# Hybrid decoder layer on one core: the first layer of the NSA compression with its tokens stationary and its weights moving

## The chip, the cores and the metric

The kernel runs on one core of one Trainium2 chip. The metric is device time in microseconds for one execution of the whole layer, from the first to the last instruction; lower is better.

## The reference, cut to what matters

One decoder layer for 512 tokens of width 1024: a joint input projection feeds multi-head latent attention (MLA) and native sparse attention (NSA: selected, sliding-window and compressed branches), an output projection and a squared-ReLU MLP follow. The change lies in the compressed branch, which turns windows of 32 tokens (stride 16, so 31 windows) of keys (kv = 0) and values (kv = 1) into one token each by a small two-layer network:

```python
def compress(t, pe, w1, w2):           # t: keys or values, 2 groups (G) x 64 (Dh)
    c = t.reshape(B, n_chunk, CMP_STRIDE, G, Dh)
    blocks = jnp.concatenate([c[:, :-1], c[:, 1:]], axis=2)
    blocks = blocks + pe[None, None, :, None, :]
    flat = blocks.transpose(0, 1, 3, 2, 4).reshape(B, n_cmp, G, CMP_BLOCK * Dh)
    return jax.nn.silu(flat @ w1) @ w2          # w1: 2048 x 128, w2: 128 x 64
k_cmp = rms_norm(compress(keys), k_gain[0]);  v_cmp = compress(values)
```

## The kernel before, in words

TensorE (PE) turns, multiplies and accumulates in PSUM; ScalarE (ACT) and VectorE (DVE) split float32 operands into a high and a low fp32r half, run the softmax and empty PSUM; GpSimd (POOL) does inverse roots, row scalings and the DMAs that add; SyncE (SP) loads weights. Each weight slice ("piece") of 128 x 1024 float32 goes through one of three slots of `raw` (RAW = 3) in the order of PIECES (L109), so that piece n may be loaded only when piece n - 3 is done with (`raw_free`, L592).

The attention is a list of units (UNITS, L156). Engines run the loop over units n in step with each other: at step n, PE computes the scores of unit n (`score_unit`, it waits for DVE's `lows` of unit n - 2), then whatever else is put at that step, then the products with the values of unit n - 4 (`mix_unit`, or `mix_pair` for four units together, L2342), then it turns the probabilities of unit n - 2 (`turn_unit`, by the helper `turn`, L2133, which waits for ACT's exponential). DVE at step n adds bias and finds the maximum (L1568) and copies turned probabilities (L1580); ACT runs the exponential of unit n - 1 (L1119). The first 32 units are MLA's; u = n - 32 counts NSA's. This order is written out by hand.

Compression is dealt out to the steps by `compress(u)` on each engine:
- u = 0, 2, 4, 6 on PE: the raw keys and values of 128 tokens are turned; ACT (`top_taps`, L1205) and DVE (`low_taps`, L1722) copy them at u = 1, 3, 5, 7 to `tap_planes`, where partitions 0 to 63 hold a token and 64 to 127 the next one. A row of position embeddings stands at either end.
- u = 10 to 17 on PE: `hidden(kv, quarter)` (L2378), the first layer. w1 is stationary (128 x 128), the 64 windows (2 groups x 32) move past it. Four matmuls a visit, keys at u = 10 to 13, values at u = 14 to 17. Each takes a half of w1: pieces w1 0 and 1 are the halves for keys, 2 and 3 for values. Piece 0 is free after the visit at u = 11 (`taps_used`), piece 1 after the visit at u = 13 (`turned`).
- u = 14 and 18 on DVE: the sums are put together (L1764 to L1771); u = 15 and 19 on ACT: the exponential (L1252); u = 16 and 20, 21 on DVE: 1 + e, its reciprocal and the product, `hid_k` and `hid_v` (L1776 to L1789).
- The second layer: keys on PE at u = KC_AT = 19 (L2261), DVE's `kc_ss` at u = 19 (L1733 to L1737), POOL's inverse root, PE again at KT_AT = 25; values at VC_AT = 27. The compressed keys are first used at u = 28.

Between these steps PE turns MLA's output rows (`turn_mix`, MIX_AT: u = 9, 15, 20, 23; made by POOL's `mix_row_of`), and from u = 21 on it runs parts of the output projection at most steps (L2113 to L2115).

A float32 matmul (not fp32r) shows in the trace as two LDWEIGHTS and two MATMUL records; a float32 transposition as one of each.

## Time and profile before

| | |
|---|---|
| Median of 3 runs | 641.41 us (640.96 to 641.7) |
| The profiled execution's own time | 640.96 us |
| Its span | 639.1 us |
| Granted TensorE clock, mean | 1.0 of full speed |
| PE busy | 626.0 us (98%) |
| DVE busy | 496.3 us (78%) |
| ACT busy | 400.0 us (63%) |
| POOL busy | 172.3 us (27%) |

The profiled execution is one of the three. Shares are of the span; busy times of one engine are the union of its instructions, and a "xN" is a count of records.

### The profile page before, as it was taken

What the parts mean: (1) busy time and instruction counts of PE and PEld (TensorE: products, weight loads), DVE (VectorE), ACT (ScalarE), POOL (GpSimd) and SP (SyncE); (2) the same over time, 40 slices, a digit from 0 to 9 for tenths busy, and PEclk for the clock granted to TensorE, in tenths of its full rate; (3) what the DMA queues carried; (4) which work ended last, traced back from release to release, by engine and by line L of the source; (5) the groups of instructions that cost most, each with busy time, mean ns of one, the idle gap of its engine ahead of it and who ended that gap; (6) DMA issues with size and microseconds to landing.
All of it is one profiled execution on the core that took longest, in us unless ns stands there. A gap on an engine that the chain in (4) does not pass through costs nothing.

```text
span 639.1 us, 11631 instructions
## 1 busy us (share of the span) xinstructions
PE 626.0 (98%) x4105; PEld 553.2 (87%) x4105; DVE 496.3 (78%) x913; ACT 400.0 (63%) x791; POOL 172.3 (27%) x236
## 2 busy tenths in 40 slices
PE   7999999999999999999999999999999999999998
PEld 5999788887689888888899999999998788888886
DVE  6665756578887888887896787777778999987666
ACT  5864675567897647566457676666747566644462
POOL 5656656434322201122110111111112121222200
PEclk9999999999999999999999999999999999999999
DMA  9881629997998964897365688787877899999975
GB/s 337 279 307 71 260 69 341 301 286 209 248 269 253 367 205 165 264 265 165 55 145 183 174 222 236 194 220 203 205 175 170 211 237 241 241 222 257 258 233 174
DMA packets 34506, 142.49 MB, mean 223 GB/s; under 512 B 5159, under 2 KB 5543, under 8 KB 33488
## 3 DMA queue, kind: packets, MB, share of 16 engines
q1 hardware_dynamic: 22688, 83.72, 37.8%
q0 software_dynamic: 10208, 34.88, 29.5%
q10 hardware_dynamic: 1552, 23.14, 9.5%
q8 instruction: 33, 0.54, 0.3%
q14 instruction: 25, 0.20, 0.1%
HBM read 139.57 MB, written 65.06 MB: 320 GB/s over the span
## 4 chain that ended last, share of the span: by engine, by line
PE 87%; DVE 5%; ACT 3%; DMA 3%; issue 2%; POOL 1%; SPq 0%; ACTq 0%; DVEq 0%; POOLq 0%
PE bank L2113 15%; PE bank L2115 15%; PE bank L2114 15%; PE bank L2503 7%; PE bank L2505 7%; PE bank L2504 7%; PE bank L2133 7%; PE bank L2342 3%; PE bank L2285 2%; PE bank L2324 2%; DVE w_lo L1396 1%; PE bank L2296 1%; PE bank L2297 1%; DMA raw<-weights 1%; PE bank L2378 1%
## 5 line engine op out<-in xcount | busy, mean ns | idle before, releaser
L868 POOL DMA_DIRECT2D down_sums<-w_down x64 | 49.8, 779 | 230.8 <-PE bank L2505 138.8
L1396 DVE TENSOR_TENSOR w_lo<-raw,w_hi 128x1024 fp32r<-128x1024 f32 (+3 forms) x70 | 81.1, 1171 | 22.9 <-ACT w_hi L965 22.5
L2113 PE MATMUL bank<-w_hi,act_hi 128*128 128x512 f32 (+3 forms) x224 | 89.6, 400 | 3.0 <-DVE w_lo L1396 2.6
L965 ACT ACTIVATE w_hi<-raw 128x1024 fp32r<-128x1024 f32 (+3 forms) x70 | 68.5, 993 | 30.4 <-DMA raw<-w_pairs 22.5
L2115 PE MATMUL bank<-w_hi,act_lo 128*128 128x512 f32 (+3 forms) x224 | 79.7, 356 | 0.0
L2114 PE MATMUL bank<-w_lo,act_hi 128*128 128x512 f32 (+3 forms) x224 | 79.7, 356 | 0.0
L1119 ACT ACTIVATE p_buf<-s_buf,stats 128x128 f32<-128x128 f32 (+3 forms) x96 | 53.8, 561 | 32.3 <-PE bank L2133 17.3
L1357 ACT ACTIVATE w_hi<-raw 128x1024 fp32r<-128x1024 f32 x31 | 32.8, 1059 | 35.5 <-DMA raw<-down_sums 20.7
L2113 PE MATMUL bank<-w_hi,s_all 128*128 128x512 f32 x140 | 54.7, 390 | 0.0
L2114 PE MATMUL bank<-w_lo,s_all 128*128 128x512 f32 x140 | 54.5, 389 | 0.0
L2115 PE MATMUL bank<-w_hi,s_all 128*128 128x512 f32 x140 | 54.5, 389 | 0.0
L2113 PEld LDWEIGHTS bank<-w_hi,act_hi 128*128 128x128 f32 x224 | 42.2, 188 | 13.0 <-issue 5.1
L2503 PE MATMUL bank<-act_hi,w_hi 128*128 128x256 f32 x168 | 47.6, 283 | 1.6 <-DVE a_all L1908 1.6
L2505 PE MATMUL bank<-act_hi,w_lo 128*128 128x256 f32 x168 | 47.6, 283 | 0.0
L2505 PE MATMUL bank<-g_all,w_lo 128*128 128x256 f32 x168 | 47.6, 283 | 0.0
L2503 PE MATMUL bank<-g_all,w_hi 128*128 128x256 f32 x168 | 47.6, 283 | 0.0
L2504 PE MATMUL bank<-act_lo,w_hi 128*128 128x256 f32 x168 | 47.6, 283 | 0.0
L2504 PE MATMUL bank<-g_all,w_hi 128*128 128x256 f32 x168 | 47.5, 283 | 0.0
L2114 PEld LDWEIGHTS bank<-w_lo,act_hi 128*128 128x128 f32 x224 | 42.3, 189 | 5.9 <-issue 1.2
L2115 PEld LDWEIGHTS bank<-w_hi,act_lo 128*128 128x128 f32 x224 | 42.1, 188 | 5.4
L1996 DVE TENSOR_TENSOR w_lo<-raw,w_hi 128x1024 fp32r<-128x1024 f32 x31 | 37.8, 1218 | 11.0 <-ACT w_hi L1357 11.0
L2133 PE MATMUL bank<-consts,p_buf 128*128 128x128 f32 x248 | 45.0, 279 | 1.0 <-ACT m_k L1068 0.3
(317 smaller groups left out, 1809.1 us busy)
## 6 DMA issues: line engine op xcount, KB each, us to landing
down_sums<-w_down ACTq DMA_DIRECT2D x32, 512.0 KB, 6.0
down_sums<-w_down POOLq DMA_DIRECT2D x64, 256.0 KB, 5.6
raw<-down_sums SPq DMA_DIRECT2D x32, 512.0 KB, 5.4
up_sums<-w_pairs POOLq DMA_DIRECT2D x28, 512.0 KB, 9.3
raw<-up_sums SPq DMA_DIRECT2D x28, 512.0 KB, 4.6
raw<-weights SPq DMA_DIRECT2D x26, 512.0 KB, 6.3
up_sums<-w_pairs SPq DMA_DIRECT2D x16, 512.0 KB, 6.4
raw<-w_down SPq DMA_DIRECT2D x16, 512.0 KB, 5.2
```

Of the source, the lines that this page charges most:

```text
L868: pool.dma_start(sums_dram[k, rows_], a["w_down"][SUMS[m][1], step, rows_], accum_op=ALU.add, max_dma_last_dim=4096).then_inc(*sum_added[k ...
L965: ins = act.activation(hi[:, 0:width], raw[:, n % RAW, 0:width], ACT.Copy)
L1119: act.activation(p_buf[:, n % 2, 0:nk], s_buf[:, n % 2, 0:nk], ACT.Exp, scale=-1.0, bias=neg_max[:, m:m + 1], accum_out=den[:, d:d + 1]).t ...
L1396: ins = dve.tensor_tensor(lo[:, 0:width], raw[:, n % RAW, 0:width], hi[:, 0:width].bitcast(F32), ALU.subtract)
L1996: dve.tensor_tensor(lo, src, hi.bitcast(F32), ALU.subtract).then_inc(*lo_done.mark(JOBS[d]))
L2113: pe.matmul(dst, a_h, w_h, start=start, stop=False, skip_group_check=onto)
L2114: pe.matmul(dst, a_h, w_l, start=False, stop=False, skip_group_check=onto)
L2115: return pe.matmul(dst, a_l, w_h, start=False, stop=stop, skip_group_check=onto)
L2133: ins = pe.transpose(bank[0:m, i * step:i * step + k], tile, ident[0:k, 0:k])
L2503: pe.matmul(dst, h[:, k * P:(k + 1) * P], g_h[:, k, :], start=start and k == 0, stop=False, skip_group_check=onto)
L2504: pe.matmul(dst, h[:, k * P:(k + 1) * P], g_l[:, k, :], start=False, stop=False, skip_group_check=onto)
L2505: ins = pe.matmul(dst, l[:, k * P:(k + 1) * P], g_h[:, k, :], start=False, stop=k == KD // 2 - 1, skip_group_check=onto)
```

## The change

Stationary and moving change places. A matmul now has 64 windows (for one kv) as its stationary operand, 128 x 64, read from `tap_planes` at every 8th element, and 128 columns of w1 move. Keys' sums go to partitions 0 to 63 of a PSUM bank, values' to 64 to 127, the two alternating as `mix_pair` does. The eight visits become four, at u = 10, 11, 13 and 14, of eight matmuls each (four for keys, four for values); the visits at 10 and 11 take both first halves of w1, those at 13 and 14 both second halves, and the pieces are ordered so. ACT copies the sums (128 x 256) to `hid_rows` at u = 15, PE turns them at u = 16 (two transpositions), DVE's and ACT's steps and the keys' second layer move back by one to four steps. `tap_planes` holds only even tokens above and odd ones below, so that the copies are half as wide, with PSUM read at every second element. POOL's `mix_row_of(0, 3)` is moved ahead of the keys' inverse root.

```diff
-KC_AT, VC_AT, KT_AT = 19, 27, 25
+HID_AT, HID_COPY, HID_TURN, HID_SUM, HID_EXP = (10, 11, 13, 14), 15, 16, (17, 18), (18, 19)
+HID_RATIO = ((19, 19), (20, 21))
+KC_AT, VC_AT, KT_AT = 21, 27, 25
...
+        hid_rows = place("hid_rows", 256, at=r_onsa)
...
-            return turned.at(("hid", i // 2)) if i % 2 else taps_used.at(n)
+            return taps_used.at(i // 2)
...
             for t in range(3):
                 mix_row_of(0, t)
             add_up(12, 2)
+            mix_row_of(0, 3)
             pool.wait_ge(*dve_step.at("kc_ss"))
             rsqrt("kc", kc_rs[0:64, :], kc_ss[0:64, :], HD)
-            mix_row_of(0, 3)
             add_up(14, 2)
...
-                bank = TD[bank_of("T", ("taps", t))][:, 0:2 * P].rearrange("p (j s) -> p j s", j=2)
+                bank = TD[bank_of("T", ("taps", t))][:, 0:2 * P].rearrange("p (kv c l o) -> p kv c l o", kv=2, l=8, o=2)
                 for i in range(2):
-                    act.activation(tap_planes[0:HD, 2 * i:2 * i + 2, CMP_STRIDE + t * P:CMP_STRIDE + (t + 1) * P], bank[HD * i:HD * i + HD, :, :],
+                    act.activation(tap_chunks[0:HD, :, 1 + 8 * t:9 + 8 * t, i, :], bank[HD * i:HD * i + HD, :, :, :, 0],
                                    ACT.Copy).then_inc(*copied.mark(("taps", t, i)))
...
-                if u in (15, 19):
-                    kv = (u - 15) // 4
+                if u == HID_COPY:
+                    act.wait_ge(*taps_used.at(1))
+                    act.activation(hid_rows, TD[bank_of("T", "hid")][:, 0:256], ACT.Copy).then_inc(*copied.mark("hid"))
+                if u in HID_EXP:
+                    kv = HID_EXP.index(u)
...
-                if u in (14, 18):
-                    kv = (u - 14) // 4
-                    dve.wait_ge(*turned.at(("hid", kv)))
+                if u in HID_SUM:
+                    kv = HID_SUM.index(u)
+                    dve.wait_ge(*turned.at("hid turned"))
...
-            def hidden(kv, quarter):
...
-                bank = TD[known["bank", "T", ("hid", kv)]]
-                n = PIECE_AT["w1", 2 * kv + quarter // 2]
-                pe.wait_ge(*raw_in[n % RAW].at(n))
-                for i in range(4 * (quarter % 2), 4 * (quarter % 2) + 4):
-                    lp = 8 * (quarter // 2) + i
-                    w = raw[:, n % RAW, i * P:(i + 1) * P]
-                    at = 2 * lp + CMP_STRIDE * (lp // 8)
-                    tok = tap_planes[:, kv:4:2, at:at + CMP_STRIDE * (NC - 1) + 1:CMP_STRIDE]
-                    half = lp // 8
-                    ins = pe.matmul(bank[:, 2 * NC * half:2 * NC * half + 2 * NC], w, tok, start=lp % 8 == 0, stop=lp % 8 == 7)
-                if quarter == 1:
-                    ins.then_inc(*taps_used.mark(n))
-                if quarter == 3:
-                    ins.then_inc(*turned.mark(("hid", kv)))
+            def hidden(visit):
...
+                half, lps = visit // 2, range(4 * visit, 4 * visit + 4)
...
+                pieces = [PIECE_AT["w1", 2 * half + kv] for kv in range(2)]
+                for n in pieces:
+                    pe.wait_ge(*raw_in[n % RAW].at(n))
+                for lp in lps:
+                    at = lp % 8 + 2 * CMP_STRIDE * half
+                    for kv in range(2):
+                        tok = tap_planes[:, kv, at:at + 8 * (2 * NC - 1) + 1:8]
+                        w = raw[:, pieces[kv] % RAW, (lp % 8) * P:(lp % 8 + 1) * P]
+                        ins = pe.matmul(bank[64 * kv:64 * kv + 64, P * half:P * half + P], tok, w, start=lp % 8 == 0, stop=lp % 8 == 7)
+                if visit % 2:
+                    ins.then_inc(*taps_used.mark(half))
...
-                if 10 <= u < 18:
-                    hidden((u - 10) // 4, (u - 10) % 4)
+                if u in HID_AT:
+                    hidden(HID_AT.index(u))
+                if u == HID_TURN:
+                    pe.wait_ge(*copied.at("hid"))
+                    turn("hid turned", [hid_rows[:, P * half:P * half + P] for half in range(2)], (dve_step, ("z", 1)), kind="D")
...
-            part = chunks(v["nsa_cmp_w1"][0, i // 2, 8 * P * (i % 2):8 * P * (i % 2 + 1)])
+            part = chunks(v["nsa_cmp_w1"][0, i % 2, 8 * P * (i // 2):8 * P * (i // 2 + 1)])
```

Where the rows stand in PE's order, steps u = 12 and 13. Before (scores L2296 and L2297, visits L2378, turned probabilities L2133; `raw_in0` to `raw_in2` are the landings in the three slots of `raw`, and piece w1 3 goes to slot 1 again):

```order
L2296 MATMUL bank<-act_hi,q_pairs_103 128x512 [waits lows]
L2297 MATMUL bank<-act_lo,q_pairs_103 128x512
L2378 MATMUL bank<-tap_planes,raw 128x64 [waits raw_in2]
L2378 MATMUL bank<-tap_planes,raw 128x64 x3
L2133 MATMUL bank<-consts,p_buf 128x128 [waits act_pt,probs]
L2133 MATMUL bank<-consts,p_buf 128x128 x3
L2296 MATMUL bank<-act_hi,q_pairs_103 128x512 [waits lows]
L2297 MATMUL bank<-act_lo,q_pairs_103 128x512
L2378 MATMUL bank<-tap_planes,raw 128x64 [waits raw_in2]
```

The same two steps in the changed kernel:

```order
L2300 MATMUL bank<-act_hi,q_pairs_104 128x512 [waits lows]
L2301 MATMUL bank<-act_lo,q_pairs_104 128x512
L2137 MATMUL bank<-consts,p_buf 128x128 [waits act_pt,probs]
L2137 MATMUL bank<-consts,p_buf 128x128 x3
L2300 MATMUL bank<-act_hi,q_pairs_104 128x512 [waits lows]
L2301 MATMUL bank<-act_lo,q_pairs_104 128x512
L2381 MATMUL bank<-raw,tap_planes 64x128 [waits raw_in1,raw_in0]
L2381 MATMUL bank<-raw,tap_planes 64x128 x7
```

The visit at u = 12 is gone, and the one at u = 13 takes slots 1 and 0, pieces w1 3 and w1 2, where before it took slot 2, piece w1 1.

DVE's order at steps u = 18 to 20 of the changed kernel (L1575 are the bias steps of units 18, 19 and 20, L1587 copies turned probabilities of units 15 and 17):

```order
L1587 COPY pt_x<-bank 128x512 [waits mixed,turned]
L1575 ISA s_buf,stats<-bank,bias 128x384 [waits probs,scores]
L1770 COPY stats<-bank 128x1 [waits turned]
L1772 TENSOR_TENSOR stats<-bank,stats 128x1 [waits dve_step]
L1775 TENSOR_SCALAR z_buf<-bank,stats 128x62 [waits dve_step]
L1777 TENSOR_TENSOR z_buf<-bank,z_buf 128x62 [waits dve_step]
L1575 ISA s_buf,stats<-bank,bias 128x384 [waits probs,scores]
L1781 TENSOR_SCALAR z_buf<-z_buf 128x62 [waits exp_small]
L1785 RECIPROCAL z_buf<-z_buf 128x62 [waits dve_step]
L1791 TENSOR_TENSOR hid_k<-z_buf 128x2x31 [waits pool_step,dve_step]
L1587 COPY pt_buf<-bank 128x384 [waits mixed,turned]
L1575 ISA s_buf,stats<-bank,bias 128x384 [waits probs,scores]
```

`hid_k` stood at step 16 before and now stands at step 19, and PE's matmul that waits for it moved from step 19 to step 21.

## Rows read from the trace of the kernel before

**Rows 1.** The page, part 1, PE.

```profile
PE 626.0 (98%) x4105; PEld 553.2 (87%) x4105; DVE 496.3 (78%) x913; ACT 400.0 (63%) x791; POOL 172.3 (27%) x236
```

**Rows 2.** Busy time by window: length, PE, PEld, DVE, ACT, POOL, PEclk, DMA share, GB/s.

```profile
194.40:198.30 3.90, 3.90 (x50) 3.65 (x49) 2.54 (x7) 3.85 (x10) 2.98 (x5) 1.00 0.68 209
198.30:204.30 6.00, 6.00 (x50) 5.69 (x48) 5.40 (x16) 4.53 (x13) 0.00 (x0) 1.00 1.00 272
204.30:216.10 11.80, 11.80 (x127) 10.76 (x126) 8.11 (x28) 6.42 (x17) 2.14 (x6) 1.00 1.02 361
```

**Rows 3.** Timeline of PE, steps u = 10 to 13 and 21: start, length, instruction.

```profile
191.57 1.04 PE L2378 MATMUL bank<-tap_planes,raw 128*128 128x64 f32 x8
192.44 0.62 PE L2133 MATMUL bank<-consts,p_buf 128*128 128x128 f32 x4
...
193.36 1.05 PE L2378 MATMUL bank<-tap_planes,raw 128*128 128x64 f32 x8
194.34 1.97 PE L2342 MATMUL bank<-pt_x,n_v 128*64 128x128 f32 x32
196.24 0.66 PE L2133 MATMUL bank<-consts,p_buf 128*128 128x128 f32 x4
196.65 0.47 PE L2296 MATMUL bank<-act_hi,q_pairs 128*128 128x512 f32 x1
...
198.98 1.06 PE L2378 MATMUL bank<-tap_planes,raw 128*128 128x64 f32 x8
...
216.15 0.47 PE L2113 MATMUL bank<-w_hi,act_hi 128*128 128x512 f32 x1
```

**Rows 4.** Chain that ended last: MLA scores (512 moving columns), `mix_pair`, four records of 64 moving columns.

```profile
154.22 0.86 PE bank L2285 x2
...
204.47 1.90 PE bank L2342 x32
...
254.28 0.45 PE bank L2324 x4
```

**Rows 5.** Instructions of the tile tap_planes: ns of one (min/median/max).

```profile
L2378 PEld LDWEIGHTS bank<-tap_planes,raw x64: 187/192/193, 191.3 to 209.5; 128*128 128x128 f32 x64
L1205 ACT ACTIVATE tap_planes<-bank x8: 361/374/381, 176.7 to 187.3; 64x256 f32<-64x256 f32 x8
L1722 DVE COPY tap_planes<-bank x8: 416/422/429, 177.1 to 188.3; 64x256 f32<-64x256 f32 x6, 64x254 f32<-64x254 f32 x2
```

**Rows 6.** DMA issues and landing: window 194.0 to 194.7 (w1 2).

```profile
raw<-weights SPq DMA_DIRECT2D x1, 512.0 KB, 4.4
```

**Rows 7.** Line L727 in the window 195.5 to 196.3 (w1 3): issue and landing.

```profile
L727 SPq DMA_DIRECT2D raw<-weights x1: 1320/1320/1320, 194.8 to 194.8; - x1
...
DMA to landing us min/median/max: 9.5/9.5/9.5
```

**Rows 8.** The page, part 6: all loads of weights, median us to landing.

```profile
raw<-weights SPq DMA_DIRECT2D x26, 512.0 KB, 6.3
```

**Rows 9.** Timeline of DVE, steps u = 16, 18 and 19.

```profile
207.60 0.55 DVE L1568 CUSTOM_DVE_ANT_0 s_buf<-bank,bias 128x384 f32<-128x384 f32 x1
...
208.08 0.19 DVE L1776 TENSOR_SCALAR z_buf<-z_buf 128x62 f32<-128x62 f32 x1
208.30 0.54 DVE L1781 RECIPROCAL z_buf<-z_buf 128x62 f32<-128x62 f32 x1
208.88 0.23 DVE L1787 TENSOR_TENSOR hid_k<-z_buf 128x62 f32<-128x62 f32 x1
...
211.42 0.15 DVE L1764 COPY stats<-bank 128x1 f32<-128x1 f32 x1
...
212.25 0.55 DVE L1568 CUSTOM_DVE_ANT_0 s_buf<-bank,bias 128x384 f32<-128x384 f32 x1
```

**Rows 10.** Timeline of ACT's queue: a copy of weights in DRAM, issued at u = 14.

```profile
200.62 0.50 ACTq L688 DMA_DIRECT2D down_sums<-w_down  x1
```

**Rows 11.** Timeline of PE: the first matmuls of the span.

```profile
1.45 5.04 PE L2215 MATMUL bank<-warm 128*128 128x512 f32 x6 [1.45 <-DVE warm L1445]
7.68 0.41 PE L2113 MATMUL bank<-w_hi,act_hi 128*128 128x384 f32 x1 [1.20 <-DVE w_lo L1396]
```

More of the change, by code:

```diff
@@ L404, in build @@
         nq_row = place("nq_row", 512, at=base + 14336)
-        tap_planes = place("tap_planes", 4 * TAP, at=r_mk).rearrange("p (j s) -> p j s", j=4)
+        tap_planes = place("tap_planes", 2 * TAP, at=r_mk).rearrange("p (kv n) -> p kv n", kv=2)
+        tap_chunks = tap_planes.rearrange("p kv (c g l) -> p kv c g l", g=2, l=8)
         bias_ct = place("bias_ct", 2 * SEQ, at=r_mk + 4 * TAP * 4).rearrange("p (g s) -> p g s", g=2)
@@ L1716, in low_taps @@
             def low_taps(t):
[L1718 to L1719 removed]
+                bank = TD[bank_of("T", ("taps", t))][:, 0:2 * P].rearrange("p (kv c l o) -> p kv c l o", kv=2, l=8, o=2)
                 for i in range(2):
                     dve.wait_ge(*copied.at(("taps", t, i)))
[L1722 to L1723 removed]
+                    dve.tensor_copy(tap_chunks[HD:P, :, 1 + 8 * t:9 + 8 * t, i, :],
+                                    bank[HD * i:HD * i + HD, :, :, :, 1]).then_inc(*dve_step.mark(("taps", t, i)))
             def mix_lows(g, t):
@@ L1755, in compress @@
                     pe = const("pe").rearrange("p (kv half l) -> p half kv l", kv=2, half=2)
-                    for half, at in enumerate((0, CMP_STRIDE + SEQ)):
+                    for half, at in enumerate((0, NC + 1)):
                         for g in range(2):
-                            ins = dve.tensor_copy(tap_planes[:, 2 * g:2 * g + 2, at:at + CMP_STRIDE:2], pe[:, half])
+                            ins = dve.tensor_copy(tap_chunks[:, :, at, g, :], pe[:, half])
                     ins.then_inc(*dve_step.mark("pe_rows"))
-                if u in (14, 18):
-                    kv = (u - 14) // 4
-                    dve.wait_ge(*turned.at(("hid", kv)))
-                    sums = TD[bank_of("T", ("hid", kv))][:, 0:4 * NC].rearrange("p (half g c) -> p half g c", half=2, g=2)
+                if u in HID_SUM:
+                    kv = HID_SUM.index(u)
+                    dve.wait_ge(*turned.at("hid turned"))
+                    sums = TD[bank_of("T", "hid turned")][:, 0:8 * NC].rearrange("p (half kv c g) -> p half kv g c", half=2, kv=2, g=2)[:, :, kv]
                     dve.tensor_copy(pe_lo[:, kv:kv + 1], sums[:, 0, 0, 0:1]).then_inc(*dve_step.mark(("pe_lo", kv)))
@@ L1771, in compress @@
                     dve.tensor_tensor(z, sums[:, 1, :, 0:N_CMP], z, ALU.add).then_inc(*dve_step.mark(("z", kv)))
-                if u in (16, 20):
-                    kv = (u - 16) // 4
+                for kv in [kv for kv in range(2) if HID_RATIO[kv][0] == u]:
                     dve.wait_ge(*exp_small.at(kv))
@@ L1776, in compress @@
                     dve.tensor_scalar(e, e, 1.0, None, ALU.add).then_inc(*dve_step.mark(("e1", kv)))
-                if u in (16, 21):
-                    kv = (u - 16) // 5
+                for kv in [kv for kv in range(2) if HID_RATIO[kv][1] == u]:
                     e = z_buf[:, 1, kv, :]
```

15 lines of the change are left out of this document (6 added, 9 removed).

## The prediction

> **What bounds the kernel now.** The page's first part comes first: PE is busy for 98% of the span, DVE for 78%, so TensorE sets the time unless a place says otherwise [rows 1]. Next I read the busy time in windows around the change. From 194.4 to 216.1 PE has no gap at all, in the three windows one after the other, while ACT and DVE have room after 198.3; the DMA engines, though, are full from 198.3 on (share 1.00 and 1.02) [rows 2]. So PE's work here counts one for one, and a transfer asked for here is slow. Later stages are PE's too (98% leaves little), and what SyncE loads there waits for slots that PE's progress frees, so I let a shift at 216 us pass to the end unchanged.
>
> **The visits of the first layer.** The timeline shows what one costs: the visit that starts at 191.57 is followed at 192.44, so eight records take 0.87 us, 0.109 each [rows 3]. The weight load of 128 columns, 192 ns long and back to back, goes with it [rows 5]. Eight visits are 8 x 0.87 = 6.96 us. The new visit has the form of a `mix_pair` block: 128 x 64 stationary, 128 columns moving, halves of the array in turn. Such a block of 32 records takes 1.90 us, 0.059 each [rows 4]. The new visit has 16 records, 0.95 us; four are 3.80. That removes 3.16 us. The two transpositions at u = 16 are half of the four that take 196.65 - 196.24 = 0.41 us [rows 3]: 0.2 added. **PE's own work falls by 2.95 us.**
>
> **The wait that the change makes.** The visit at u = 13 used w1 piece 1; now it uses pieces 2 and 3. Piece 3 goes to the slot of piece 0, which is free only after the visit at u = 11, before and after. Its load was issued at 194.8, and landed 9.5 us later, at 204.3 [rows 7]; before, it was wanted at u = 16, after 206.7, and nobody waited. Piece 2, issued at 194.4, took 4.4 us and is there at 198.8 [rows 6]. Now PE reaches u = 13 at 198.98 [rows 3], less the visit left out at u = 12 (0.87), plus twice 0.08 for the longer ones before: 198.27. The landing: 0.1 to 0.2 us later by the issue, but sooner by some tenths, because ACT's copy of weights at 200.62 [rows 10] sits behind an exponential that waits for a turn which PE does after this visit, so its traffic is missing during the wait. I take 204.0: **PE waits 5.7 us.** The bounds: 0.9 if the load took the 4.4 us of its neighbour [rows 6], 2.8 at the 6.3 us that is the median of all weight loads [rows 8], 8 if it took some 12 us. I take the row of this very load, for the queue ahead of it and the full DMA engines stay. Behind PE's wait stands everything: the turn of unit 11's probabilities, then ACT's exponential of unit 13. DVE and ACT catch up, but what they catch up is not PE's time. The piece after (output weights) is now issued at once behind the two loads of x, where it waited for u = 13 before; it is behind piece 3 on the same queue, is used much later, and I cost it at nothing. That holds unless queues share badly, which the upper bound of the landing takes in.
>
> **The later steps of DVE.** DVE's two groups of sums (four small instructions each, starting at 211.42 and done before 212.25, some 0.9) and its ratio for the keys (0.19 + 0.54 + 0.23 from 208.08, done by 209.02) now all fall on u = 17 to 19 [rows 9]. From the bias step of unit 16 (207.60) to that of unit 19 (212.25) were 4.65 us; with the ratio out and the second group of sums in they are 4.6, then 0.6 for unit 19 and 0.95 for the ratio: `hid_k` about 6.2 us after unit 16's bias step begins. PE had 7.8 us from the end of unit 16's scores (207.1) to the scores of u = 21 (about 214.9); without two visits (1.74) and the second-layer matmul (0.3), with the turn (0.2), it has 6.0, and the bias step starts up to 0.5 after the scores. So PE waits for `hid_k` at u = 21 for some tenths, and perhaps at the products of u = 19, which take a copy of DVE's that is later. I take 0.6 us, between 0 and 1.2. From 216.15 [rows 3] on PE has output projection between its steps, and DVE's lag is covered by it.
>
> **Edits with no cost.** The copies to `tap_planes` are half as wide: eight of 374 ns and eight of 422 ns [rows 5], which can only become shorter (none to 0.3 us of PE, before the wait, so it moves the load as well as PE). ACT's new copy of 256 columns stands in ACT's room in the third window (6.42 busy of 11.80) [rows 2], 0.4 us, done under the products of step 15. On POOL the moved row is made earlier, and the keys' root has three steps before DVE reads it; the two adding DMAs behind it start some 4 us later and are read some 100 us later.
>
> **Sum:** -2.95 + 5.7 + 0.6 = +3.35 us. The profiled execution took 640.96, so 644.3; it lies 0.45 below the median of 641.41, so **644.8 us** for the median.
>
> **The rivals.**
> *TensorE's clock falls in the wait (28%).* Before, PE has no gap like it, so no row shows the clock in one. But rows show the engine at the lower of its two levels: the first six matmul records, after idling, take 5.04 us, 0.84 each, at 1.2 GHz [rows 11], where two float32 records of scores with as many moving columns take 0.86 us, 0.43 each [rows 4]; at 7.68, when the next matmul comes, it is at 2.4 GHz, 384 columns in 0.41 us [rows 11]. The granted clock reads 1.00 there too, so durations tell, not that column. If 5.7 us of rest have the same effect, some 5 us of elapsed time go at half speed: 2.5 us lost, of which 0.6 covers DVE's lag: +5.25, **646.7**. The Trainium skill, "TensorE: Matmul & The Clock Gate", in its table on why this matters, says that a gap between bursts of matmuls drops the clock to half until work restores it; by that rule this case would be the forecast. I keep it second because no row here shows a fall within the run.
> *The load is faster (13%).* At the median of 6.3 us [rows 8] it lands at 201.1: -2.95 + 2.8 + 0.6 = +0.45, **641.9**, no difference that can be told. Against it: the DMA share of 1.00 in that window.
> *Faster after all (7%).* Piece 3 lands like piece 2, within 4.4 us [rows 6], at 199.2, and DVE keeps up: -2.95 + 0.9 = -2.05, **639.4**. It decides at a landing by 199.3 with DVE's 0.6, which leaves a gain of 1.3. For it speaks only that one neighbour, which had the engines nearly to itself.
> *The change does not do what it says (5%).* The stationary operand is read at every 8th element, 32 bytes apart; `mix_pair` reads it side by side. If loads then take double, a record is again 0.109 and a visit 1.74: PE's work is +0.2, the load is issued 1.7 later (lands at 206.0), PE arrives at 199.85: +0.2 + 6.2 + 0.6 = +7.0, **648.4**. Against it: before, 64 moving columns were read 64 bytes apart at 0.109 a record, and 64 columns side by side take 0.45 for four, 0.112 [rows 4]. The Trainium skill, "SBUF — State Buffer", section "Door 1: The DMA port swizzle", says that float32 reads more than four elements apart lose bandwidth; by that rule this rival would be the case. The trace of the moving operand does not show the loss, and of the stationary one no run here shows anything.
>
> **The numbers.** Forecast (644.8) 42%, clock 28%, faster load 13%, faster 7%, slow loads 5%, something between or beyond 5%. About 0.2%, 1.3 us, is what a measurement of this kernel can tell from no change. Faster by more: 7%. Within: 13%. Slower: 80%. The range goes from 641.2, a little under the faster load, to 648.0, past the clock's case with a landing a microsecond late. The forecast's own range is 643 to 646.5.
>
> **What would show it.** Right: in PE's timeline a gap before the third visit, of 4 to 7 us, put down to the DMA of weights; visits of 0.95 us; a short wait before the keys' second layer; PE busy some 3 us less and idle some 6 more. The clock's case: matmuls with 512 moving columns after the gap twice as far apart as before it. Wrong: no such gap, or a gap below 2 us; visits of 1.7 us; a wait that appears later, at the output projection or at the first compressed scores.

## The result and the profile after

| | before | changed |
|---|---|---|
| Median | 641.70 us (11 runs, 640.96 to 644.28) | 646.57 us (11 runs, 643.64 to 649.38) |
| The profiled execution's own time, its span | 640.96, 639.1 us | 644.08, 642.2 us |
| Granted TensorE clock, mean, of that one | 1.000 | 0.994 |

The ratio is 1.007, with a 95% interval of 1.0052 to 1.0088: the change costs some 0.7%. The median lies 1.8 us above the 644.8 predicted, within the range. Two things stand out beside it: the changed kernel's runs are spread over 5.7 us, and the execution with the profile is one of its fastest, 2.5 us under the median. So this profile shows what happens, and probably understates how much of it there is in a usual run. Its mean granted clock of 0.994 holds two falls: one behind the gap that is shown below, and one in the first matmuls (0.82 over 8 to 12 us, 0.76 over 12 to 16), where the kernel before stood at 1.00. The mean clock of a run is therefore no measure of this change alone.

The page of the changed kernel, part 1, answers to [rows 1]: PE is busy for about as long as before, in a span that is 3.1 us longer.

```profile
PE 625.6 (97%) x4107; PEld 552.9 (86%) x4107; DVE 496.7 (77%) x913; ACT 398.6 (62%) x792; POOL 172.6 (27%) x236
```

PE's timeline of the changed kernel from the first visit (L2381) over the third and on to the place where [rows 3] ended; start, length, instruction, and in brackets the idle time before it and what ended it:

```profile
190.29 1.25 PE L2381 MATMUL bank<-raw,tap_planes 128*64 128x128 f32 x16
191.47 0.65 PE L2137 MATMUL bank<-consts,p_buf 128*128 128x128 f32 x4
...
197.06 0.40 PE L2301 MATMUL bank<-act_lo,q_pairs 128*128 128x512 f32 x1
201.62 1.99 PE L2381 MATMUL bank<-raw,tap_planes 128*64 128x128 f32 x16 [4.16 <-DMA raw<-weights]
203.54 1.11 PE L2137 MATMUL bank<-consts,p_buf 128*128 128x128 f32 x4
204.45 0.92 PE L2354 MATMUL bank<-consts,o_t 128*128 128x128 f32 x4
205.12 0.47 PE L2300 MATMUL bank<-act_hi,q_pairs 128*128 128x512 f32 x1
...
211.19 0.38 PE L2137 MATMUL bank<-consts,hid_rows 128*128 128x128 f32 x2
211.41 0.60 PE L2137 MATMUL bank<-consts,p_buf 128*128 128x128 f32 x4
...
213.53 0.55 PE L2137 MATMUL bank<-consts,p_buf 128*128 128x128 f32 x3 [0.39 <-ACT p_buf L1123]
...
219.25 0.47 PE L2117 MATMUL bank<-w_hi,act_hi 128*128 128x512 f32 x1
```

The gap of 4.16 us before the third visit is put down to the DMA of weights. A visit that is not behind the gap starts 1.18 us before what follows it (190.29 to 191.47), the one behind it 1.92 us (201.62 to 203.54), and the four transpositions after that 0.91 us, where 0.41 was usual [rows 3]. The last row started at 216.15 before, so this place is 3.10 us later, and the span is longer by the same 3.1.

Windows of 2 us around the gap in the changed kernel (length, PE, PEld, DVE, ACT, POOL, granted PE clock, DMA share, GB/s):

```profile
198.00:200.00 2.00, 0.00 (x0) 0.00 (x0) 1.53 (x4) 1.28 (x5) 1.26 (x2) 1.00 0.94 260
200.00:202.00 2.00, 0.38 (x4) 0.41 (x6) 0.00 (x0) 0.00 (x0) 0.00 (x0) 0.92 1.13 379
202.00:204.00 2.00, 2.00 (x18) 1.67 (x15) 0.00 (x0) 0.00 (x0) 0.00 (x0) 0.50 0.92 258
204.00:206.00 2.00, 2.00 (x14) 1.64 (x14) 0.82 (x2) 0.81 (x2) 0.00 (x0) 0.73 1.09 285
```

The granted clock falls near the end of PE's rest, is at half (1.2 of 2.4 GHz) while PE works again, and is on its way back in the last window (1.00 from 206 on). ACT and DVE, which wait for PE's products, stand still from 202 to 204: nobody uses the gap.

The line that loads weights, in the window 193.6 to 194.3, is piece w1 3 and answers to [rows 7]:

```profile
L731 SPq DMA_DIRECT2D raw<-weights x1: 603/603/603, 193.8 to 193.8; - x1
...
who waited for it (us, times):
  PE bank L2381: 4.2, 1
...
DMA to landing us min/median/max: 7.7/7.7/7.7
```

It took 7.7 us here, where it had taken 9.5. The instructions of the tile `tap_planes` answer to [rows 5]:

```profile
L2381 PEld LDWEIGHTS bank<-raw,tap_planes x64: 194/213/226, 190.3 to 206.6; 128*64 128x64 f32 x64
...
L1209 ACT ACTIVATE tap_planes<-bank x8: 254/267/275, 176.3 to 186.2; 64x128 f32<-64x128 f32 x8
L1728 DVE COPY tap_planes<-bank x8: 283/290/295, 176.5 to 187.0; 64x128 f32<-64x128 f32 x8
```

The copies are a third shorter (374 to 267 ns, 422 to 290 ns). The weight load of only 64 columns, though, takes 213 ns at the median, no less than the 192 ns of the 128 columns before.

### The profile page after: what moved, and what is told of

Read it like the earlier page. It is cut to its first block, busy times and chain, and to the rows that moved or that the text cites. A ratio compares the mean times of both kernels' runs of the same rounds, so it can differ in the third digit from the quotient of the medians.

```text
span 642.2 us, 11640 instructions
## 1 busy us (share of the span) xinstructions
PE 625.6 (97%) x4107; PEld 552.9 (86%) x4107; DVE 496.7 (77%) x913; ACT 398.6 (62%) x792; POOL 172.6 (27%) x236
## 4 chain that ended last, share of the span: by engine, by line
PE 88%; DVE 5%; ACT 3%; DMA 2%; issue 1%; ACTq 0%; DVEq 0%
PE bank L2117 15%; PE bank L2119 15%; PE bank L2118 15%; PE bank L2507 7%; PE bank L2137 7%; PE bank L2508 7%; PE bank L2509 7%; PE bank L2346 3%; PE bank L2289 2%; PE bank L2328 2%; DVE w_lo L1403 2%; PE bank L2300 1%; PE bank L2301 1%; DMA raw<-weights 1%; PE bank L2381 1%
```

## The experiments

Twelve kernels, measured in four groups (e1 to e4, e5 to e8, e9 to e11, e12), each with the kernel before beside it. Theory A: the wait that the change makes, with the clock's fall in it, is its whole price, and the rest of the change gains. The rivals are in the expectations. Medians of the kernel before differ by a microsecond between groups, so ratios are what to compare. A ratio is an estimate of its own and not the quotient of the two medians; in e7 the two differ by 0.3% (1.0042 against 1.0074), in the others by at most 0.25%.

| kernel | median (lowest to highest) | before | ratio [95%] |
|---|---|---|---|
| e1, no second late piece | 638.92 (638.05 to 641.63) | 641.28 | 0.9972 [0.9959, 0.9984] |
| e2, wait filled | 644.07 (642.40 to 645.34) | 641.28 | 1.0035 [1.0020, 1.0050] |
| e3, narrow planes alone | 640.71 (639.43 to 641.97) | 641.28 | 0.9977 [0.9962, 0.9992] |
| e4, planes side by side | 644.53 (640.90 to 648.75) | 641.28 | 1.0065 [1.0041, 1.0090] |
| e5, load alone | 644.68 (642.10 to 650.97) | 641.93 | 1.0038 [1.0008, 1.0069] |
| e6, visits two later | 644.34 (640.66 to 646.47) | 641.93 | 1.0020 [0.9997, 1.0044] |
| e7, visits one later | 646.66 (639.16 to 649.59) | 641.93 | 1.0042 [1.0010, 1.0074] |
| e8, e6 with planes side by side | 645.82 (641.48 to 646.97) | 641.93 | 1.0036 [1.0014, 1.0058] |
| e9, a piece for a visit | 639.03 (638.01 to 641.72) | 640.80 | 0.9975 [0.9959, 0.9990] |
| e10, other traffic moved | 640.43 (639.09 to 2969.93) | 640.80 | 0.9992 [0.9981, 1.0004] |
| e11, e9 and e10 | 638.92 (637.95 to 640.49) | 640.80 | 0.9970 [0.9959, 0.9981] |
| e12, POOL's traffic moved | 642.89 (640.42 to 646.37) | 641.86 | 1.0018 [1.0000, 1.0037] |

One of e10's twelve executions took 2970 us, for a reason that no record here shows; the other eleven lie between 639.09 and 642.27.

### e1: both visits of the second half read one piece

```diff
-            return taps_used.at(i // 2)
+            return raw_in[n % RAW].at(n) if i == 3 else taps_used.at(i // 2)
...
-                pieces = [PIECE_AT["w1", 2 * half + kv] for kv in range(2)]
+                pieces = [PIECE_AT["w1", 2 * half + kv * (1 - half)] for kv in range(2)]
```

The values' second half is multiplied by the keys' weights here, so piece w1 3 is loaded but not read, and its slot is free as soon as it has landed.

> Both second-half visits read piece w1 2 for keys and values; piece w1 3 is loaded, but nothing on TensorE waits for it (the compressed values come from the wrong half of w1; the arithmetic is the same in size). Theory (the wait for piece w1 3 and the clock that falls in it are the loss): the gap of 4.2 us before the third visit goes, the third visit costs as much as the first (1.2 us and not 1.9), the granted clock stays at 1.0 throughout, and the time is 638 to 639 us, 2.5 to 3.5 us below the kernel before. Rival (the loss sits in the visits and the later steps, and the wait is only where they show): the gap moves to a later place and the time stays above 641 us.

Measured: 638.92, ratio 0.9972 [0.9959, 0.9984]. PE's timeline of e1 at the third visit follows the scores of its step within 0.2 us, and PE reaches at 214.19 the row that stood at 216.15 before and at 219.25 in the changed kernel:

```profile
198.06 1.24 PE L2381 MATMUL bank<-raw,tap_planes 128*64 128x128 f32 x16
199.23 0.65 PE L2137 MATMUL bank<-consts,p_buf 128*128 128x128 f32 x4
...
214.19 0.47 PE L2117 MATMUL bank<-w_hi,act_hi 128*128 128x512 f32 x1
```

Without the late piece the change is faster than the kernel before, by the ratio 1.8 us where 2.5 to 3.5 were expected: the whole loss, and more, hangs on that one wait.

### e2: PE kept busy in the wait

```diff
+                if visit == 2:
+                    for _ in range(18):
+                        pe.matmul(bank[:, 2 * P:3 * P], ident, ident, start=True, stop=True)
                 for n in pieces:
                     pe.wait_ge(*raw_in[n % RAW].at(n))
```

The added matmuls write to a part of the bank that nothing reads.

> The changed kernel with 18 matmuls of 128 x 128 by 128 columns (36 records, about 3.9 us) into unused columns of the same bank, just before the third visit's wait. Theory (the clock falls because TensorE rests): the wait shrinks to under 1 us, the clock stays at 1.0, the third visit takes 1.2 us, and the time is 1 to 1.5 us below the changed kernel's 646.6. If the clock costs nothing, the time is that of the changed kernel or some tenths more. If TensorE was resting for a reason that is not the load, the time rises by 3.9 us.

Measured: 644.07, ratio 1.0035 [1.0020, 1.0050]. PE's timeline:

```profile
197.66 4.18 PE L2376 MATMUL bank<-consts 128*128 128x128 f32 x36
203.50 1.25 PE L2384 MATMUL bank<-raw,tap_planes 128*64 128x128 f32 x16 [1.67 <-DMA raw<-weights]
204.68 0.66 PE L2137 MATMUL bank<-consts,p_buf 128*128 128x128 f32 x4
```

In this execution the piece took 9.2 us and PE could not go on for 5.84 us (197.66 to 203.50), 1.7 more than in the changed kernel's profile. That the wait left over is 1.67 us, and not under 1 as expected, comes from this late landing. But the granted clock stays 1.00 in every window from 192 to 216, and the visit behind takes 1.18 us and not 1.92. Against the changed kernel the median is 2.5 us less, and by the two ratios 0.35%, or 2.2 us, is gained. I take that for the price of the fallen clock in a usual run; it is an estimate, since the two kernels were measured in different groups and the landings of their unprofiled runs are not seen. The spread shrinks from 5.7 to 2.9 us.

### e3: the narrow planes alone, in the kernel before

```diff
-                    act.activation(tap_planes[0:HD, 2 * i:2 * i + 2, CMP_STRIDE + t * P:CMP_STRIDE + (t + 1) * P], bank[HD * i:HD * i + HD, :, :],
+                    act.activation(tap_chunks[0:HD, :, 1 + 8 * t:9 + 8 * t, i, :], bank[HD * i:HD * i + HD, :, :, :, 0],
...
-                    tok = tap_planes[:, kv:4:2, at:at + CMP_STRIDE * (NC - 1) + 1:CMP_STRIDE]
+                    tok = tap_planes[:, kv, at:at + 8 * (2 * NC - 1) + 1:8]
```

> The kernel before with only the new planes: even tokens above, odd ones below, copies half as wide. Theory (the 1.3 us that TensorE is ahead at the first visit, 190.3 against 191.6, come from the shorter copies): the time is 1.0 to 1.4 us below the kernel before. Rival (I had costed the copies at nothing to 0.3 us): within 0.3 us of the kernel before.

Measured: 640.71, ratio 0.9977 [0.9962, 0.9992]. The tile in e3 against [rows 5]:

```profile
L2378 PE MATMUL bank<-tap_planes,raw x64: 276/298/303, 190.4 to 208.8; 128*128 128x64 f32 x64
L1206 ACT ACTIVATE tap_planes<-bank x8: 254/268/273, 176.4 to 186.4; 64x128 f32<-64x128 f32 x8
```

From the first of ACT's copies to the first visit are 13.95 us (176.4 to 190.35), where 14.9 were before (176.7 to 191.57) and 14.0 are in the changed kernel (176.3 to 190.29): the shorter copies bring 0.9 us. Laid row by row beside the kernel before, PE steps ahead at three places, by 0.35 us at 178, 0.2 at 185 and 0.45 at 188.9, each time at the first matmuls behind one of DVE's copies to `tap_planes`. The visits take 0.93 instead of 0.87 us, so eight of them give back 0.5.

Against the expected 1.0 to 1.4 us the time says little: the median is 0.6 us below the kernel before, the ratio means 1.5 us. The profiled execution is the slowest of its twelve, and it shows where such a difference comes from. Every profile of these kernels has a rest of PE of 1.5 to 1.8 us near 350; in thirteen of fourteen the granted clock stays 1.00 behind it, in this one it falls, over 16 matmuls that take 3.4 us instead of 1.9. PE's row of e3 and its windows 348 to 352 and 352 to 356:

```profile
351.62 0.36 PE L2503 MATMUL bank<-act_hi,w_hi 128*128 128x256 f32 x1 [1.82 <-DVE a_all L1908]
```

```profile
348.00:352.00 4.00, 2.18 (x19) 2.01 (x18) 3.66 (x6) 1.39 (x3) 0.00 (x0) 1.00 0.64 178
352.00:356.00 4.00, 4.00 (x23) 4.00 (x23) 3.13 (x5) 3.08 (x5) 0.00 (x0) 0.57 0.23 80
```

This has nothing to do with the change. It is one of the ways in which runs of all these kernels come to differ by a microsecond or two.

### e4: the planes laid out by element, so that 64 stationary columns lie side by side

```diff
-        tap_chunks = tap_planes.rearrange("p kv (c g l) -> p kv c g l", g=2, l=8)
+        tap_chunks = tap_planes.rearrange("p kv (l c g) -> p kv c g l", g=2, l=8)
...
-                    at = lp % 8 + 2 * CMP_STRIDE * half
+                    at = (lp % 8) * 2 * (NC + 2) + 4 * half
...
-                        tok = tap_planes[:, kv, at:at + 8 * (2 * NC - 1) + 1:8]
+                        tok = tap_planes[:, kv, at:at + 2 * NC]
```

> The changed kernel with planes laid out so that the 64 stationary columns stand side by side in memory and not 32 bytes apart; copies of the same size write at a wider step. Theory (the stride costs the weight load: 213 ns a record where mix_pair's takes 137, and 0.074 us a record where mix_pair takes 0.059): LDWEIGHTS of 137 ns, visits of 0.95 us at full clock, 0.7 to 1.0 us less than the changed kernel. Rival (the stride costs nothing, the visits are slow for another reason): 213 ns and 1.2 us as before.

Measured: 644.53, ratio 1.0065 [1.0041, 1.0090], not to be told from the changed kernel. The tile's rows:

```profile
L2381 PEld LDWEIGHTS bank<-raw,tap_planes x64: 132/137/231, 190.6 to 204.8; 128*64 128x64 f32 x64
...
L1209 ACT ACTIVATE tap_planes<-bank x8: 381/396/413, 175.8 to 186.4; 64x128 f32<-64x128 f32 x8
L1728 DVE COPY tap_planes<-bank x8: 382/392/401, 176.2 to 187.3; 64x128 f32<-64x128 f32 x8
```

The weight load comes down from 213 to 137 ns and a visit from 1.18 to 1.02 us (190.63 to 191.65), 0.064 a record. But the copies that write this layout take 396 and 392 ns, and from the first copy to the first visit are 14.8 us again. What four visits gain, 0.64, the copies lose, 0.8. Its gap was 2.56 us, with the piece landing after 6.1 us, and the clock fell in that too (0.74 on the mean of 198 to 204).

### e5: the third piece of the output weights loaded behind w1

```diff
-    add("wo", 3, 1024)
+    add("wo", 2, 1024)
     add("w1", 4, 1024, False)
-    add("wo", 8, 1024, first=3)
+    add("wo", 8, 1024, first=2)
...
-WO_SPLIT = {0: 17 - N_MLA, 1: 27 - N_MLA, 2: 9, 3: 26, 4: 31, 5: 33, 6: 35, 7: 39}
+WO_SPLIT = {0: 17 - N_MLA, 1: 27 - N_MLA, 2: 24, 3: 26, 4: 31, 5: 33, 6: 35, 7: 39}
```

> The changed kernel, with the third piece of the output weights loaded after the four pieces of w1 instead of before them (its split on ACT and DVE at step 24 instead of 9). w1 piece 2 then goes to a slot that is free much earlier, and piece 3 follows the same last visit as before, but with no 512 KB of piece 2 beside it. If the wait at u = 13 is the transfer's own time behind full DMA engines (theory A), the landing comes down from 7.7 us to about 4.4 to 5.5, PE waits 1 to 2 us instead of 4.2, the clock hardly falls, and the time is 641 to 642.5. If the landing is set by the neighbours' traffic on the other queues (rival B: down weights and x), piece 3 takes its 7 to 8 us again, the wait stays near 4 and the time near 646. A granted clock under 1.00 after a wait of 1 to 2 us would say that even that is enough to lose it.

Measured: 644.68, a miss on the time. Where it was aimed it did what theory A says: the piece landed 3.8 us after its issue at 195.0, PE waited 0.25 us, and at 215.03 PE was 1.1 us ahead of the kernel before. Then a new wait comes. Windows of e5, and behind them the row of PE's timeline in the first of them:

```profile
234.00:240.00 6.00, 3.18 (x18) 2.25 (x16) 3.35 (x9) 0.76 (x2) 0.00 (x0) 0.89 0.54 217
240.00:246.00 6.00, 6.00 (x43) 4.89 (x42) 3.76 (x12) 1.89 (x7) 0.00 (x0) 0.83 0.27 87
```

```profile
237.84 0.52 PE L2137 MATMUL bank<-consts,p_buf 128*128 128x128 f32 x3 [2.65 <-DVE pt_buf L1587]
```

PE waits there for a copy of DVE's, and DVE in its turn for a transfer. DVE's timeline of e5:

```profile
236.54 0.69 DVE L1817 TENSOR_TENSOR x<-bank,x 128x512 f32<-128x512 f32 x1 [4.42 <-DMA x<-x]
237.15 0.55 DVE L1587 COPY pt_buf<-bank 128x384 f32<-128x384 f32 x1
```

I had moved the piece's split to step 24 and costed that at nothing. Until its split the piece keeps its slot of `raw`, so the load that takes the slot next is issued only at 227.2. The two reloads of x stand behind that load on SyncE's queue: they are issued at 227.6 and 229.4, where the changed kernel issues them at 216.4 and 216.7, and the second lands 7.0 us later, when DVE has stood for 4.42 us. PE rests 2.8 us of the first window and the clock falls: a row of PE's that stood at 242.90 before is at 246.44, so 4.7 us are lost since the row at 215.03. So e5's time says nothing of the load; its trace does. It is the same fault as the changed kernel's, at another place: a transfer that lands behind its reader, and PE at rest.

### e6 and e7: the third and fourth visits at u = 15 and 16, or at 14 and 15

```diff
-HID_AT, HID_COPY, HID_TURN, HID_SUM, HID_EXP = (10, 11, 13, 14), 15, 16, (17, 18), (18, 19)
-HID_RATIO = ((19, 19), (20, 21))
-KC_AT, VC_AT, KT_AT = 21, 27, 25
+HID_AT, HID_COPY, HID_TURN, HID_SUM, HID_EXP = (10, 11, 15, 16), 17, 18, (19, 20), (20, 21)
+HID_RATIO = ((21, 21), (22, 23))
+KC_AT, VC_AT, KT_AT = 23, 27, 25
```

(e7: visits (10, 11, 14, 15), copy 16, turn 17, sums (18, 19), exponentials (19, 20), ratios ((20, 20), (21, 22)), KC_AT 23.)

> The changed kernel, its third and fourth visits at u = 15 and 16 instead of 13 and 14, and all that follows them two steps later (copy 17, turn 18, sums 19 and 20, exponentials 20 and 21, ratios 21 to 23, the keys' second layer at 23). PE reaches u = 15 at about 202.5, a microsecond after the landing (201.5) of the profiled run. If the wait and the clock's fall in it are all that the change costs (theory A), both go: clock 1.00 in 198 to 210, no wait for w1, and with the gains (copies 1.3, visits 2.2, less two transpositions) about 3 us faster than before: 637.7 to 639.5. If half of the cost came from DVE's crowded steps or from the visits' own length (rival B), 640 to 642.

> The changed kernel, its third and fourth visits at u = 14 and 15, all that follows one step later (the keys' second layer at 23). PE reaches u = 14 about 2 us later than u = 13, at 199.5 to 200: where the load lands at 201.5 it waits 1.5 to 2 us, where it lands late, 3 to 6. Theory A (each microsecond of wait counts, and the clock falls in the longer ones): 640 to 642.5, between the changed kernel and the one with visits two steps later, with a wide spread over its runs, a part of them with a clock under 0.995. Rival B (the wait's length does not matter, only that there is one): 644 or more.

Measured: 644.34 and 646.66; both still wait. The waits of PE, e6 and then e7:

```profile
PE bank L2381 <- DMA raw<-weights: 3.3, 1, 3.3
```

```profile
PE bank L2381 <- DMA raw<-weights: 5.4, 1, 5.4
```

Two errors of mine: the visits that are taken away from u = 13 and 14 also take away their own 2.4 us, so PE came to u = 15 at 200.1 and not at 202.5 (203.36, the start of the visit, less 3.25); and I took 201.5 for the landing, which was the lucky 7.7 us. In e6 the piece took 9.8 us, in e7 10.2. e7's twelve runs are the clearest picture: two without a fall of the clock, at 639.16 and 640.53 (granted clock 1.000), and ten at 646.4 to 649.6 (0.989 to 0.995). The same program is either under the median of the kernel before or 0.7 to 1.2% above it. That the landing decides which is what e9 and e10 then bear out; no run but the profiled one shows its own.

### e8: e6 with e4's layout

The edits are those of e6 and e4.

> As the kernel with visits two steps later, and in addition tap_planes laid out by element, so that the 64 stationary columns of one record lie side by side. One look at this layout in the changed kernel showed the weight load at 137 ns instead of 213 and a visit at 1.02 us instead of 1.18, but the copies that write it at 396 and 392 ns instead of 267 and 290. So PE gains 4 x 0.16 = 0.64 us in the visits and gives back about 0.35 before the first one: 0.3 us less than the kernel with visits two steps later, if theory A holds there (637.4 to 639.2). If the layout's gain were all of the visits' 0.64, 0.6 less; if the copies cost more than that, 0 to 0.5 more.

Measured: 645.82, a miss, and no better than e6. The piece took 10.7 us and PE waits 3.9 us for it, so it says little of the layout.

### e9: w1 packed by visit

```diff
-            return taps_used.at(i // 2)
+            return taps_used.at(i)
...
-                pieces = [PIECE_AT["w1", 2 * half + kv] for kv in range(2)]
-                for n in pieces:
-                    pe.wait_ge(*raw_in[n % RAW].at(n))
+                pe.wait_ge(*raw_in[n % RAW].at(n))
...
-                        w = raw[:, pieces[kv] % RAW, (lp % 8) * P:(lp % 8 + 1) * P]
+                        w = raw[:, n % RAW, (4 * kv + lp % 4) * P:(4 * kv + lp % 4 + 1) * P]
...
-            part = chunks(v["nsa_cmp_w1"][0, i % 2, 8 * P * (i // 2):8 * P * (i // 2 + 1)])
+            part = np.concatenate([chunks(v["nsa_cmp_w1"][0, kv, 4 * P * i:4 * P * (i + 1)]) for kv in range(2)], axis=1)
```

Here n is PIECE_AT["w1", visit], `taps_used` is marked at every visit, the visits stand at u = 10, 11, 13 and 16, and what follows stands as in e6.

> The changed kernel with w1 packed by visit: each 512 KB piece holds the four weight blocks of one visit for keys and for values, so a visit reads one piece, and piece 3's slot is free after the visit at u = 10, not 11. The third visit stays at u = 13, the fourth goes to u = 16, what follows goes two steps later (keys' second layer at 23). Theory A (the new wait for the late load, with the clock's fall in it, is what the change costs, and its visits and copies gain some 3 us): piece 2, asked for at 193 as before, is there by 197.5 to 199, so a wait of 0 to 1.5 us at u = 13; piece 3 has until about 204.5, and it took until 201.5 to 203.7 in the four kernels profiled; clock 1.00 between 198 and 210; 638 to 640, ratio 0.995 to 0.998, and a narrower spread than the changed kernel's. Rival B (the landing times of both pieces grow with the traffic whatever their order): waits of 2 us or more at u = 13, and 642 or more.

Measured: 639.03, ratio 0.9975 [0.9959, 0.9990]: faster than the kernel before, and by the two ratios 0.9% faster than the changed kernel. PE's timeline:

```profile
196.94 1.25 PE L2379 MATMUL bank<-raw,tap_planes 128*64 128x128 f32 x16
...
203.78 1.26 PE L2379 MATMUL bank<-raw,tap_planes 128*64 128x128 f32 x16
...
207.27 0.41 PE L2137 MATMUL bank<-consts,hid_rows 128*128 128x128 f32 x2 [0.51 <-ACT hid_rows L1255]
...
212.72 0.48 PE L2117 MATMUL bank<-w_hi,act_hi 128*128 128x512 f32 x1
```

The loads of weights issued at 192.6 and 193.0 took 4.3 and 9.9 us, as slow as ever, and landed at 196.9 and 202.9. PE comes to the third visit just as piece 2 lands and to the fourth 0.9 us behind piece 3: PE has no wait for weights in its table of waits, and the granted clock is 1.00 from 192 to 216. The transfer was not made faster; its deadline was put behind it. A lead of 0.9 us is little against landings that differ by more, and three of the ten runs lie above 640.4. The 0.51 us for `hid_rows` is the price of my placing: the turn stands one step behind ACT's copy.

### e10 and e12: the traffic of the other queues moved away

```diff
+_moved = [UNIT_COPIES.pop(32 + 8 + 2 * _i) for _i in range(8)]
+UNIT_COPIES.update({32 + 16 + _i: _copy for _i, _copy in enumerate(_moved)})
...
-            add_up(12, 2)
             mix_row_of(0, 3)
             pool.wait_ge(*dve_step.at("kc_ss"))
             rsqrt("kc", kc_rs[0:64, :], kc_ss[0:64, :], HD)
-            add_up(14, 2)
+            add_up(12, 4)
```

e10 has both edits, e12 only the second.

> The changed kernel with the other traffic of 188 to 204 us taken away from the load of piece 3: ACT's copies of down weights at u = 8 to 22 go one to a step to u = 16 to 23, and POOL's pair of adding transfers (issued at 194.5) goes behind the keys' root. If the DMA engines' sharing sets the landing (theory A), piece 3 lands about 4.4 us after it is asked for, at 198 to 199, PE waits 1 to 1.5 us instead of 4.2, the clock hardly falls, and the time is 641 to 643.5 with a narrower spread. If the load takes its time alone or behind its neighbour on SP's queue (rival B), it still lands 7 us or more after the issue, and the time stays at 645 to 647. The traffic moved to 205 and later could cost a microsecond of its own in either case.

> The changed kernel with only POOL's pair of adding transfers (two of 512 KB, issued at 194.5 right behind the loads) moved behind the keys' root, and ACT's copies left where they are. With both moved the profiled wait for piece 3 came to 1.9 us and the time to 640.4. If POOL's adding transfers alone slow the load (theory A), the wait is 2 to 2.5 us here too and the time 640.5 to 642. If ACT's copies of down weights, issued at 190.6 and 196.4, do it (rival B), the wait stays near 4 us, the granted clock falls in it, and the time stays at 645 to 647. If each has a share, a wait near 3 us and 642 to 645.

Measured: 640.43, ratio 0.9992 [0.9981, 1.0004], and 642.89, 1.0018 [1.0000, 1.0037]. The load of piece w1 3 in e10:

```profile
L733 SPq DMA_DIRECT2D raw<-weights x1: 328/328/328, 193.4 to 193.4; - x1
...
who waited for it (us, times):
  PE bank L2382: 1.9, 1
...
DMA to landing us min/median/max: 5.4/5.4/5.4
```

5.4 us instead of 7.7 (6.1 to 10.7 in the other profiles), 1.9 us of waiting where 1 to 1.5 were expected, and a granted clock of 1.00 in all windows of this stretch. e10's windows 198 to 204, where the changed kernel's DMA share was 0.92 to 1.13:

```profile
198.00:204.00 6.00, 5.08 (x51) 4.38 (x52) 3.71 (x11) 2.18 (x7) 1.01 (x2) 1.00 0.64 250
```

In e12 the piece took 5.3 us and PE waited 1.8, at a granted clock of 1.00, in one of its lowest executions (640.53). So the other queues' transfers do delay the landing. They are not alone in it: in e5 POOL's pair (issued at 194.83) and ACT's copy (197.56) were in place, and the piece landed after 3.8 us, with no other load of weights issued just ahead of it. That is one execution. The long landings, 6.1 us and more, come in the profiles that have both the neighbour on SyncE's queue and POOL's pair. e12 takes two thirds of the way by the ratios (0.5% of 0.8%) and 60% by the medians (3.7 of 6.1 us), which is the time that was expected if each of the two has a share. But the intervals of e10 and e12 overlap, so the share of ACT's copies is likely and not shown. The Trainium skill, "DMA: Bandwidth & Descriptors", section "Issuing engines are not separate DMA queues", says that transfers started by any engine run on the same 16 DMA engines and interleave. These two runs agree.

### e11: e9 and e10 together

> Both: w1 packed by visit with visits at u = 10, 11, 13 and 16, and the other traffic moved away from its loads. If both waits are gone already with the packing alone, this adds nothing (within 0.5 us of that kernel, 638 to 640). If the packing alone leaves runs in which a piece is late, those runs go here: the highest of the runs comes down to within 2 us of the lowest. If the moved traffic is late for what reads it, or crowds the loads of 205 to 215, 1 to 2 us more.

Measured: 638.92, ratio 0.9970 [0.9959, 0.9981]. The median is e9's, and the runs lie closer: 637.95 to 640.49, 2.5 us where 2 were expected. The moved copies cost nothing that can be seen.

## Why the prediction was right, point by point

**What bounds the kernel.** Right for the changed kernel: +3.10 at the row of 216 us and +3.1 of span. In e2, e4, e10 and e12 the two agree within 0.3 us as well, in e9 (-3.4 and -2.9) and e11 within 0.6. It is no law: e1, e3 and e6 lose 1.8 to 2.1 us more behind that row (e1: -2.0 there, -0.2 at the end), e7 1.2, and no profile gains more than 0.1. The part of e3 is mostly the fall near 350; e1 and e6 have some 1 us of waits for DVE's `act_lo` that the kernel before lacks; the rest is open. Medians are the safer comparison.

**The visits.** The term was mis-sized. Eight at 0.87 became four at 1.18, which is -2.24 us and not -3.16. PE's own work falls by 2.0 us and not by 2.95. I took the 0.059 us of a `mix_pair` record for the new one's, which is 0.074. The rival of slow loads had the cause, not the size: weight loads of 213 ns against 137 side by side, and 1.18 against 1.02 us a visit (e4), 0.64 us in all and far from a doubling. The Trainium skill's sentence, in "SBUF — State Buffer", section "Door 1: The DMA port swizzle", that strides past four float32 elements lose bandwidth is borne out by this for the stationary operand. For the moving operand e3 does not bear it out: both its strides are past four elements, and the shorter one, 32 bytes, took 0.93 us a visit where 64 bytes took 0.87.

**The two transpositions.** 0.22 us (211.19 to 211.41), as forecast.

**The wait for w1 3.** Right in place, cause and order of size: 4.16 us in the changed kernel's profile, where the load took 7.7 us, against 5.7 forecast with 9.5. In the other profiles with two loads in a row and the traffic in place the same load took 9.1 (e1), 9.2 (e2), 9.6 (e3), 6.1 (e4), 9.8 (e6), 10.2 (e7), 10.7 (e8) and 9.9 (e9): the 9.5 that I took from [rows 7] was the usual one. The changed kernel's usual run is 2.5 us above its profiled one, and e7's profile (wait 5.4, 646.77 us) shows such a run; that the changed kernel's unprofiled runs wait as long is argued from this, not seen.

**DVE's lag.** Wrong in name, near in size. No wait for `hid_k` is recorded before 217.86, where 0.6 was forecast; instead 0.39 us of waiting for ACT's exponential at 213.53, in the changed kernel and in e1, e2, e4, e5, e10 and e12 alike.

**The copies, costed at nothing.** Mis-sized: 0.9 us of gain (e3, e4), where I allowed 0.3. I saw 374 and 422 ns and did not follow the chain: turn, ACT's copy, DVE's copy, eight times over, with PE held up behind its end at three places.

**The clock.** This is the step of the forecast that failed: the sum put the clock's fall at nothing, and the rival that had it, at 28%, came true. That the rival's 646.7 is within 0.2 us of the median, and the forecast's 644.8 within 1.8, is in part luck, by errors that cancel. In the profiled execution the visit (0.75 us too long), the four transpositions (0.42) and L2354 (0.31) make 1.5 us; e2 gives some 2.2 to 2.5 us for a usual run, near the 2.5 that the rival had worked out from [rows 11]. The Trainium skill's rule, in "TensorE: Matmul & The Clock Gate", in its table on why this matters, that a gap between bursts drops the clock to half, is what this kernel's trace shows. It should have been the forecast.

**The sum.** For the place at 216 us in the profiled execution: start of the first visit -1.28 (copies -0.9, the rest a difference of the two executions that was there before the copies), visits -2.24, turns +0.22, wait +4.16, exponential +0.39, clock +1.48: +2.73 of +3.10. The missing 0.4 is missing in e1 as well (-2.24 + 0.22 + 0.39 = -1.63 against -1.16 from the first visit to that row). Row by row it lies beside these terms. The last scores ahead of a visit (L2301) are followed by it after 0.32 us, where it was 0.23, and four transpositions behind one take 0.41 instead of 0.37: +0.3 together. The records that end in the two waits count with their whole length (0.40 and 0.34 us) and not with the 0.23 and 0.18 that lay between them and the next: another +0.3. The visits, measured each by itself, gain 0.2 more than 2.24. So the new form also costs something in the matmuls next to it, 0.3 us here, and e4 has the 0.32 and the 0.41 with its columns side by side too.

Beside the forecast's sum, in the profiled execution: the visits and turns gained 0.9 us less, the copies gained 0.9 where the sum had nothing, the wait was 1.5 shorter and DVE's lag 0.2, and the clock cost 1.5 that the sum did not have. The mechanism, PE's wait for the late piece, was right; the closeness of the number leans on these.

**Faster after all.** At 7% it had the landing for its condition, and e1, e9 and e11 show that its sign was right wherever the piece is not late.

## What to carry to other kernels

When an edit makes a step read a piece earlier than before, or two pieces at once, compare the time at which the engine arrives with the issue plus the transfer's own duration under that stretch's traffic, and remember that work taken away ahead of the step brings the engine there sooner. A rest of TensorE of some microseconds is paid twice, once as a wait and again as slow matmuls behind it. The cheap cure is not a faster transfer but an order of the data (here one piece for each visit) that puts the deadline behind the landing; and when a kernel's runs spread more after a change, look for a transfer that is late only sometimes.

## What the runs showed of the hardware that was not expected

- Gaps of 5.36 (e7), 4.16 (the changed kernel), 3.25 (e6) and 2.56 us (e4) before a visit left PE at the lower clock behind them, and so did one of 2.65 us near 238 in e5; gaps of 1.90 (e10), 1.78 (e12) and 1.67 us (e2) left the granted clock at 1.00. The length of the gap does not decide alone: near 350 every profile has a gap of 1.5 to 1.8 us, and behind the 1.82 us of e3 the granted clock was 0.57, while it was 1.00 in the thirteen others.
- One load of 512 KB, asked for at the same place of the program, took 6.1 to 10.7 us behind a second load and beside POOL's pair of transfers, 5.3 to 5.5 with that pair moved away (e10, e11, e12), and 3.8 with the second load moved away (e5). The runs of a program that stands on the edge of it (e7) differ by 10 us.
- A weight load of 64 float32 columns took 213 ns with columns 32 bytes apart and 137 ns side by side (e4), so a strided load of 64 costs more than one of 128 columns at 192 ns [rows 5].
- Copies of 64 x 128 from PSUM took 267 (ACT) and 290 ns (DVE) into runs of eight elements, and 396 and 392 ns where these eight were written 68 elements apart (e4): on ACT somewhat longer than twice the elements had taken before (374 ns).
